# The S5 part of a hybrid sequence block on one core: pairs handled by row and column tiles of TensorE, two pairs at a time, with a scan in two halves and an output stored in two halves

## What is computed

```python
def s5_mixer(u, gate, ...):          # 32 groups, 16 channels -> 64 complex states
    bu = einsum("blgh,gph->lbgp", u, bb)           # complex, in two parts
    s[t] = ab * s[t-1] + bu[t]                     # associative_scan, complex
    y = einsum("lbgp,ghp->blgh", s_re, c_re) - einsum("lbgp,ghp->blgh", s_im, c_im)
    y = gelu(y + d_skip * u)
    val, gt = split(y @ glu_w + glu_b, 2)
    y = val * sigmoid(gt) * silu(gate)
    return rms_norm(y, norm_w)                     # then @ its rows of w_out
```

## Time and profile before

| | |
|---|---|
| median of 3 runs | 3209.98 us (3206.9 to 3210.56) |
| the profiled execution | 3215.24 us, of which the span is 3213.5 us |
| PE busy | 94% of the span |
| DVE, ACT, POOL busy | 45%, 35%, 23% |
| stage `stage_s5`, first work to the first gate matmul | 2213.5 to 2319.8 us of the span |

### The profile page before, as it was taken

One profiled execution on the slowest core, in us unless ns is written; L12 is line 12 of the kernel. 1 busy time (PEld: TensorE's weight loads), 2 busy tenths in 40 slices (PEclk: granted clock), 3 DMA queues, 4 the chain that ended last, 5 costly groups with the idle time before them and its releaser, 6 DMA issues. The chain is left out here.

```text
span 3213.5 us, 38614 instructions
## 1 busy us (share of the span) xinstructions
PE 3022.1 (94%) x14654; PEld 2444.8 (76%) x14654; DVE 1431.9 (45%) x2230; ACT 1120.5 (35%) x1491; POOL 751.8 (23%) x482
## 2 busy tenths in 40 slices
PE   8997999899999999999999999888899999999988
PEld 6675766688877788778887888766777888878876
DVE  4366144311145422343444333474443556546676
ACT  4354244321166412322222222252342454324333
POOL 2100101022211222122224222202532333123333
PEclk9998999899999999999999999999899999899989
DMA  3110210122211223121111112124132111222223
GB/s 134 42 40 14 60 34 24 29 62 62 73 47 44 63 63 125 44 73 39 60 52 46 39 40 65 46 79 72 27 105 99 40 33 34 105 47 67 79 92 118
DMA packets 247110, 194.04 MB, mean 60 GB/s; under 512 B 38004, under 2 KB 218564, under 8 KB 246988
## 3 DMA queue, kind: packets, MB, share of 16 engines
q1 hardware_dynamic: 244876, 191.33, 20.5%
q10 hardware_dynamic: 2112, 1.05, 0.1%
HBM read 165.78 MB, written 26.57 MB: 60 GB/s over the span
## 5 line engine op out<-in xcount | busy, mean ns | idle before, releaser
L138 POOL TENSOR_TENSOR w_low<-w_raw,w_high 128x1024 fp32r<-128x1024 f32 (+1 forms) x180 | 419.9, 2333 | 1755.0 <-ACT w_high L131 1751.9
L131 ACT ACTIVATE w_high<-w_raw 128x1024 fp32r<-128x1024 f32 (+1 forms) x180 | 179.4, 997 | 292.7 <-PE mix_banks L156 162.1
L156 PE MATMUL ffn_banks<-act_high,w_high 128*128 128x512 f32 x704 | 275.0, 391 | 4.0 <-POOLq L110 4.0
L156 PE MATMUL ffn_banks<-act_low,w_high 128*128 128x512 f32 x704 | 274.6, 390 | 0.0
L156 PE MATMUL ffn_banks<-act_high,w_low 128*128 128x512 f32 x704 | 274.6, 390 | 0.0
L156 PE MATMUL mix_banks<-act_high,w_high 128*128 128x512 f32 x640 | 253.9, 397 | 6.7 <-POOL w_low L138 4.3
L156 PE MATMUL mix_banks<-act_low,w_high 128*128 128x512 f32 x640 | 249.7, 390 | 0.0
L156 PE MATMUL mix_banks<-act_high,w_low 128*128 128x512 f32 x640 | 249.7, 390 | 0.0
L1778 PE MATMUL ffn_banks<-v_high,f_high 128*128 128x512 f32 x352 | 143.2, 407 | 18.2 <-DVE x L1958 9.8
L156 PEld LDWEIGHTS ffn_banks<-act_high,w_high 128*128 128x128 f32 x704 | 132.7, 188 | 32.2 <-POOLq L110 4.4
L1958 DVE TENSOR_TENSOR x<-x,ffn_banks 128x512 f32<-128x512 f32 x176 | 117.1, 685 | 83.3 <-PE ffn_banks L1778 83.3
(11 more groups left out here) (646 smaller groups left out, 7066.2 us busy)
## 6 DMA issues: line engine op xcount, KB each, us to landing
w_raw<-in_w_in SPq DMA_DIRECT2D x106, 512.0 KB, 4.1
w_raw<-in_ffn_up SPq DMA_DIRECT2D x44, 512.0 KB, 3.8
w_raw<-in_w_out SPq DMA_DIRECT2D x24, 512.0 KB, 3.7
v_raw<-in_ffn_down SPq DMA_DIRECT2D x11, 1024.0 KB, 5.0
decay<-acum_rows SPq DMA_DIRECT2D x16, 512.0 KB, 3.7
x_ring<-in_x SPq DMA_DIRECT2D x8, 512.0 KB, 10.7
m_part<-gate SPq DMA_DIRECT2D x8, 512.0 KB
other<-m_part SPq DMA_DIRECT2D x8, 512.0 KB, 3.8
```

Of the source, the lines that this page charges most:

```text
L131: act.activation(self.high[slot][:, 0:nk, :], self.raw[slot][:, 0:nk, :], ACT.Copy).then_inc(self.s("high", slot), 1)
L138: pool.tensor_tensor(self.low[slot][:, 0:nk, :], self.raw[slot][:, 0:nk, :], self.high[slot][:, 0:nk, :].bitcast(F32), ALU.subtract).then_ ...
L156: last = pe.matmul(out[:, h, :] if not halves else out[h], w[slot][:, k, :], x[:, k, cols], start=(n == 0), stop=(n == 3 * nk - 1))
```

## The change

- The loops of the phases are written out (no register arithmetic), and the first phase goes by groups of two pairs (`GQ = 2`, eight groups).
- The transposes read `T.AB` directly; POOL's `to_ab` is gone. ACT copies a group's four turned tiles at once, without zeroed halves.
- `inputs` uses column tiles: each matmul has 64 columns of weights and writes 64 partitions. `kernels` and the `CA` part of `outputs` use row tiles: each matmul contracts over 64 partitions, with separate banks for the two groups. The padded tile `cs` and POOL's `to_c` are gone, and `be` takes two copies over 128 partitions per pair where it took four over 64.
- DVE's operations go over a group. The scan is split: the first eight pairs are scanned after four groups are rotated, the last eight after the first two groups of `back`.
- The first two `kernels` run inside the first phase; then PE alternates `outputs(q)` and `kernels(q + 2)`.
- `Y` is stored in two halves. The first eight pairs are stored when they are kept: from ACT's queue this stands after `keep(8)` and `bands(10)` in its order.

The diff, cut to its core (the tiles' places and most of the removed loop bodies, described above, are left out):

```diff
-        quarters = lambda n: banks[:, n, :].rearrange("p (a b) -> p a b", b=P)
-        pT, pS, pM, pY = ([quarters(2 * n + s) for s in two] for n in range(4))
+        quarters = lambda n: banks[:, n, :].rearrange("p (u i b) -> p u i b", i=2, b=P)
+        pT, pS = ([quarters(4 + 2 * n + s) for s in two] for n in two)
+        pM, pY = ([banks[:, 4 * n + 2 * s:4 * n + 2 * s + 2, 0:P] for s in two] for n in two)
...
-                sp.wait_ge(sem("y_kept"), NQ + 2)
-                for j in range(0, ST, 2):
-                    sp.dma_start(core.s5_y[:, j, :].rearrange("(g h) b -> h g b", h=S5_N), Y[j * S5_N:(j + 1) * S5_N, :, :]).then_inc(sem("stored_even"), 16)
+                for part in two:
+                    sp.wait_ge(sem("y_kept"), (part + 1) * NQ // 2)
+                    own = slice(part * NQ, (part + 1) * NQ)
+                    for j in range(0, ST, 2):
+                        sp.dma_start(core.s5_y[:, j, :].rearrange("(g h) b -> h g b", h=S5_N)[:, own, :],
+                                     Y[j * S5_N:(j + 1) * S5_N, own, :]).then_inc(sem("stored_even"), 16)
...
+                def to_b(q):
+                    s = q % 2
+                    if q < 2:
+                        pool.wait_ge(sem("be_zero"), s + 1)
+                    else:
+                        pool.wait_ge(sem("pm"), q - 1)
+                    b = T.BB[:, :, q, :].unsqueeze(2).to_broadcast([P, 2, ST // 2, S5_N])
+                    for odd in two:
+                        pool.tensor_copy(be[s][:, :, odd, odd::2, :], b).then_inc(sem("be"), 1)
+
+                to_b(0)
+                to_b(1)
                 low(0)
+                to_b(2)
+                to_b(3)
                 low(1)
+                for q in range(4, NQ):
+                    to_b(q)
...
+                def turn(g):
+                    s = g % 2
+                    if g >= 2:
+                        pe.wait_ge(sem("abt"), g - 1)
+                    for u in range(GQ):
+                        for i in two:
+                            last = pe.transpose(pT[s][:, u, i, :], T.AB[:, i, g * GQ + u, :, :].rearrange("p j h -> p (j h)"), core.ident[:, :])
+                    last.then_inc(sem("ab_turned"), 1)
+
+                def inputs(g):
+                    s = g % 2
+                    pe.wait_ge(sem("abt"), g + 1)
+                    if g >= 2:
+                        pe.wait_ge(sem("t2"), g - 1)
+                    for u in range(GQ):
+                        for i in two:
+                            for r in two:
+                                last = pe.matmul(pS[s][side[r], u, i, :], abt[s][:, u, i, side[r]], T.UT[:, (g * GQ + u) * 2 + r, :], start=True, stop=True)
...
+                def kernels(q):
+                    s = q % 2
+                    pe.wait_ge(sem("be"), 2 * q + 2)
+                    if q >= 2:
+                        pe.wait_ge(sem("m"), 4 * (q - 1))
+                    n = 0
                     for i in two:
+                        for odd in two:
+                            for r in two:
+                                last = pe.matmul(pM[s][:, r, :], be[s][side[r], i, odd, :, :].rearrange("p j h -> p (j h)"),
+                                                 T.CA[side[r], i, q, 1 - odd:ST + 1 - odd, :].rearrange("p j h -> p (j h)"),
+                                                 start=(n < 2), stop=(n >= 6))
...
+                def outputs(q):
+                    s, g, u = q % 2, q // GQ, q % GQ
+                    pe.wait_ge(sem("sx"), 2 * g + 2)
+                    if q >= 2:
+                        pe.wait_ge(sem("y_kept"), q - 1)
                     for i in two:
                         for r in two:
+                            pe.matmul(pY[s][:, r, :], T.CA[side[r], i, q, 2:, :].rearrange("p j h -> p (j h)"), SX[g % 2][side[r], u, i, :],
+                                      start=(i == 0), stop=False)
+                    pe.wait_ge(sem("m"), 4 * (q + 1))
                     for r in two:
+                        last = pe.matmul(pY[s][:, r, :], M[s][:, r, :], T.UT[:, q * 2 + r, :], start=False, stop=True)
                     last.then_inc(sem("y"), 1)
...
+                turn(0)
+                for g in range(NGR):
+                    if g + 1 < NGR:
+                        turn(g + 1)
+                    inputs(g)
+                    if g == HALF_G + 1:
+                        kernels(0)
+                        kernels(1)
+                for q in range(NQ):
+                    outputs(q)
+                    if q + 2 < NQ:
+                        kernels(q + 2)
...
+                for q in range(NQ):
+                    keep(q)
+                    if q + 2 < NQ:
+                        bands(q + 2)
+                    if q == NQ // 2:
+                        store_odd(0)
+                store_odd(1)
...
+                for g in range(HALF_G):
+                    rotate(g)
+                scan(0)
                 dve.wait_ge(sem("scan"), 2)
+                for s in two:
+                    dve.memset(SX[s][:, :, :, 0:1], 0.0).then_inc(sem("sx_zero"), 1)
+                for g in range(HALF_G, NGR):
+                    rotate(g)
+                dve.wait_ge(sem("sx_zero"), 2)
+                back(0)
+                back(1)
+                scan(1)
+                dve.wait_ge(sem("scan"), 4)
+                for g in range(2, NGR):
+                    back(g)
```

More of the change, by code:

```diff
@@ L3757, in stage_s5 @@
         sums = out(NB - 1)[:, 0:NB]
[L3759 to L3776, removed]
+        side = [slice(r * S5_P, (r + 1) * S5_P) for r in two]
+        group = lambda t, g: t[:, :, g * GQ:(g + 1) * GQ, :].rearrange("p i u b -> p u i b")
+        turn_of = lambda g, i: T.rot[:, i, g * GQ:(g + 1) * GQ, :].unsqueeze(2).to_broadcast([P, GQ, 2, P])
         with nc.Block() as block:
@@ new lines, in inputs @@
+                def inputs(g):
[7 more added lines that the diff above has]
+                                last = pe.matmul(pS[s][side[r], u, i, :], abt[s][:, u, i, side[r]], T.UT[:, (g * GQ + u) * 2 + r, :], start=True, stop=True)
+                                if r == 0 and i == 1 and u == GQ - 1:
+                                    last.then_inc(sem("inputs"), 1)
+                    last.then_inc(sem("inputs"), 1)
@@ new lines, in keep, with store_odd @@
+                def keep(q):
+                    act.wait_ge(sem("y"), q + 1)
+                    act.activation(Y[:, q * 2:q * 2 + 2, :], pY[q % 2], ACT.Copy).then_inc(sem("y_kept"), 1)
+                for g in range(NGR):
+                    turned(g)
+                    if g in (2, HALF_G):
+                        split(g // HALF_G)
+                bands(0)
+                bands(1)
+                def store_odd(part):
+                    act.wait_ge(sem("y_kept"), (part + 1) * NQ // 2)
+                    own = slice(part * NQ, (part + 1) * NQ)
+                    for j in range(1, ST, 2):
+                        act.dma_start(core.s5_y[:, j, :].rearrange("(g h) b -> h g b", h=S5_N)[:, own, :],
+                                      Y[j * S5_N:(j + 1) * S5_N, own, :]).then_inc(sem("stored_odd"), 16)
@@ new lines, in scan, with back @@
+                def scan(part):
+                    own = slice(part * NQ // 2, (part + 1) * NQ // 2)
+                    dve.wait_ge(sem("zz"), (part + 1) * NGR)
+                    for i in two:
+                        dve.tensor_tensor_scan(R[:, i, own, :].rearrange("p q b -> p (q b)"), T.keep[:, own, :].rearrange("p q b -> p (q b)"),
+                                               Z[:, i, own, :].rearrange("p q b -> p (q b)"), 0.0, ALU.mult, ALU.add).then_inc(sem("scan"), 1)
+                def back(g):
+                    s = g % 2
+                    if g >= 2:
+                        dve.wait_ge(sem("sx"), 2 * (g - 1))
+                    else:
+                        dve.wait_ge(sem("zz"), 2 * NGR)
+                    dve.tensor_tensor(t1[s][:, :, :, :], group(R, g), turn_of(g, 0), ALU.mult).then_inc(sem("u1"), 1)
+                    dve.tensor_tensor(t2[s][:, :, :, :], group(R, g), turn_of(g, 1), ALU.mult).then_inc(sem("u2"), 1)
+                    dve.wait_ge(sem("u1"), g + 1)
+                    dve.wait_ge(sem("u2"), g + 1)
+                    if g >= 2:
+                        dve.wait_ge(sem("y"), GQ * (g - 1))
+                    dve.tensor_tensor(SX[s][:, :, 0, 1:], t1[s][:, :, 0, :P - 1], t2[s][:, :, 1, :P - 1], ALU.subtract).then_inc(sem("sx"), 1)
+                    dve.tensor_tensor(SX[s][:, :, 1, 1:], t1[s][:, :, 1, :P - 1], t2[s][:, :, 0, :P - 1], ALU.add).then_inc(sem("sx"), 1)
```

187 lines of the change are left out of this document (46 added, 141 removed).

## The result

| | before | after |
|---|---|---|
| median | 3210.18 us (4 runs, 3206.9 to 3210.56) | 3165.56 us (4 runs, 3163.71 to 3166.36) |
| the profiled execution | 3215.24 us, span 3213.5 | 3163.71 us, span 3162.0 |

The ratio is 0.9862, its 95% interval 0.9845 to 0.9879. That is 44.6 us in the medians, where 46.2 were forecast. A second set of runs of the same kernel gave 3164.94 us, 0.9859 (0.9842 to 0.9875).

What follows compares the result with a forecast made beforehand. Bounds by stretch: a ring of DVE and PE waits, the two scans, then PE at 3.34 us per pair. Gains 39.4 + 5.2 + 1.6 = 46.2 us give a median of 3163.8, say 3164; range 3155.5 to 3182.

Steps and rivals of the forecast that it cites:

- DVE sets the pace of the first phase: First phase: DVE limits each two-pair group at 2.2 us, 1.1 per pair instead of 1.94; PE and ACT hidden.
- Collisions with POOL: First phase: two POOL weight splits fall between DVE's operations and cost 1.6 us; bounds 0 to 4.7.
- Half scan: After four groups: first half of the scans, half of 10.8 us, takes 5.8 with the wait and two memsets.
- Tiles run in twos: `kernels` and `CA` matmuls: tiles of half the array run together, two records priced as one, 0.11 us.
- rival 2: Tiles do not run in twos here: first gate matmul at 2299, 27.6 us gained in all, 3182; chance 0.05.
- A change of shape: PE, second phase: each change between tiles and whole array costs 0.1 us more; two per pair, 0.2.
- The rest before the outputs: PE starts the first outputs after about 4 us of rest, at the lower clock, losing 1.7 us.
- A in sum: Stretch from last feed-forward matmul to first gate matmul: 39.4 us shorter.
- Tail: First gate matmul through GLU matmuls: PE's rest shrinks 5.2 us, eight slow records give 1.6; bounds 0 and 8.
- Rival 1: Emptying PSUM becomes the pace: 0.5 us more per pair, DVE's collisions 3 more; 36 us gained, 3174; chance 0.20.
- Rival 3: Early store does not help, the last landing coming no earlier: the tail's 6.8 us lost, 3171; chance 0.04.
- Rival 4: Slower: tiles follow one another and PE gets 1.2 GHz throughout; 30 us slower, 3240; chance 0.01.

Runs made afterwards that it cites:

- splits late: Changed kernel with POOL's two weight splits moved from between the rotations to behind `to_b(5)` and `to_b(8)`; 3162.00 us.
- one scan: Changed kernel with eight rotations, then one scan of 2048 elements instead of two half scans, then `back`; 3171.26 us.
- rows in line: Changed kernel with all matmuls of rows 0 to 63 before those of rows 64 to 127 in `kernels` and `outputs`; 3185.41 us.
- warm: Changed kernel plus 92 PE transposes that nobody reads, placed around `inputs(6)` and after `inputs(7)`; 3163.53 us.
- gate late: Changed kernel with ACT's silu of gate tile 1 and `split(3)` moved behind the GELUs and high copies; 3162.22 us.
- all three again: Changed kernel with all three, but splits behind `to_b(11)` and `to_b(14)`, 45 transposes instead of 52 after `inputs(7)`, `split(3)` before the fourth GELU; 3160.26 us.
- one store: Changed kernel with the whole of `Y` stored after the last pair, as before the change; 3168.75 us.
- all three: Changed kernel with the edits of splits late, warm and gate late together; 3161.97 us.
- four changes: Changed kernel with the same matmuls reordered, so PE goes between half tiles and whole array four times per pair instead of two; 3169.75 us.
- columns in line: Changed kernel with `inputs` doing all matmuls of output columns 0 to 63 before those of 64 to 127; 3165.38 us.

## Why the prediction was right, step by step

- **DVE sets the pace of the first phase**: right. A rotation without a collision takes 2.06 us (forecast 2.2), it starts 3.2 us into the stage instead of 4.3: the first eight transposes took 1.06 us, where I had priced them at the lower clock, 1.7. PE held DVE up once, by 0.50 us ahead of the second group. *Collisions with POOL*: forecast 1.6, measured 0.8 + 1.2 in the sums, 2.1 by "splits late". My lower bound of 0 for a split that falls on a scan was wrong: the one before cost the scans 2.1 us.
- **Half scan**: forecast 5.8 with its wait, measured 4.6. The step that failed was halving: those scans waited out a subtraction, and without one they take 8.74 (one scan), half of it 4.4. The wait and the memsets, put at 0.4, took 0.1. First outputs at 29.5 us into the stage instead of 31.5.
- **Tiles run in twos**: right. The two rows' records start 0.007 us apart, and the next two start 0.112 after them. That is rival 2 fallen; rows in line shows that they need not even be neighbours.
- **A change of shape**: mis-sized. I read only the first interval after a change and took 0.1 more. The two intervals behind each change are both long (0.20 and 0.21 us instead of 0.112): 0.19 in the changed kernel, 0.20 by the run with four. The Trainium skill states in TensorEngine Tiling (Array Packing), Key Properties, that a change of the tiling mode drains TensorE. The 0.19 agrees with that better than with my 0.1; by that rule I had put it at 0.17. The 0.14 for waits was not needed, so the pair came out at 2.18 where 2.1 was forecast: 16 x 0.112 + 2 x 0.19.
- **The rest before the outputs**: mis-sized. Forecast 1.7, measured 4.17 + 3.24 - 2 x 2.18 = 3.05, confirmed by "warm". I had taken the length of the slow stretch from the earlier trace rows, one run of sixteen records; here it lasts into the second pair.
- **Second scan covered**: right, and worth 4.1 us (one scan).
- **Store on ACT**: forecast 1.6, measured 0.5 (PE's 0.33 for ACT's `m`, and 0.17 more). ACT's issues took 3.3 us, but its copies ran between and beside them, and it had 10 us to spare in 30.
- **A in sum**: forecast -39.4, measured -40.4. The parts up to the first outputs were too dear by 2 us, the rest too cheap by 1. Single terms missed by 0.4 to 1.4 us in both directions, so that A came out within 1 us is partly luck.
- **Tail**: -4.8 for -5.2 and -1.6 for -1.6. Right in mechanism too: ACT's order holds the first GELU at 24.9 us behind the first gate matmul, as forecast, and moving it (gate late, all three again) takes the rest away.
- **Behind the stage I counted nothing**: +1.55 in the output projection, below, and +0.4 behind it, whose cause I have not found. The stage gained 46.8 us, 0.6 more than forecast; with these two it is 44.8.
- **Rival 1** (emptying PSUM): fallen, ACT is busy 20.5 of 30.3 us. **Rival 3**: fallen by "one store". **Rival 4**: the clock was low only for 6.3 us of the outputs.

## What to carry to other kernels

Price a change between tiles of 64 rows and the whole array at 0.2 us, about two records of 128 columns, and group matmuls by shape before refining anything else. Before taking a duration for an estimate, look at what ran beside it on POOL, and take the other engine's instruction out before halving or scaling it. An engine that rests before its busy stretch starts that stretch slowly; filler work ahead of it can pay, but each gain moves the next producer (here POOL's copies, then its splits) onto the path.

## What the runs showed of the hardware

- TensorE starts matmuls of one row half ahead of matmuls of the other that stand before them in its order, over at least three records and across lines (rows in line).
- DVE and POOL take turns in some pairs of instructions, and the loser waits until the other's instruction is over. DVE's sums of SBUF data, 0.42 us alone, took 1.23, 1.65 and 2.57 us beside a subtraction of 2.4 to 2.6 us, and each ended 0.28 us after it (2215.30 after 2215.02, 2227.47 after 2227.19, in "all three" 2245.58 after 2245.30). So a sum loses what is left of the subtraction when it starts. A subtraction that met two scans ran between them (one scan): 6.53 us instead of 2.35 for it, 10.8 instead of 8.74 for them. Products that read PSUM stayed at 0.69. POOL's four copies (L3817) took 3.55 us in the changed kernel beside the scan, where they take 1.00 at the stage's start, with DVE at rest.
- In the output projection eight matmuls of 512 columns run at the lower clock in eight of the thirteen profiles (0.43 us from start to start; 0.23 is usual), in the changed kernel 1.5 us after sixteen one-column matmuls and a rest of 0.26:

```profile
2365.00:2369.40 4.40, 4.40 (x13) 3.40 (x13) 0.75 (x1) 1.06 (x1) 2.21 (x1) 0.61 0.02 4
```
```profile
2365.76 0.62 PE L3949 MATMUL s_banks<-w_high,s_part_high 128*128 128x512 f32 x1
2366.18 0.63 PE L3949 MATMUL s_banks<-w_high,part_low 128*128 128x512 f32 x1
```

In the kernel before, and in one store, gate late, four changes and columns in line, the same instructions run at full clock and the stretch takes 46.87 us. In the 15 us from 2350 to 2365 gate late has the same busy time of PE as the changed kernel (14.03 and 14.02 us) and still keeps its clock. So the amount of work just ahead doesn't decide; what does stays open. Nor is it known how often either case comes in the runs that were not profiled.
